# A streaming encoder layer: the sources of three output projections transposed by VectorE and DMA in place of TensorE

## What is computed

```python
def retention_out(o, rg, g_ret, w_ret_o):
    o = rmsnorm(o, g_ret)...                    # per head
    return einsum('btv,vd->btd', silu(rg) * o, w_ret_o)

def diff_out(o, g_sub, lam_init, w_diff_o, dtype):
    o = rmsnorm(o, g_sub) * (1.0 - lam_init)
    return einsum('btv,vd->btd', o, w_diff_o)

def gated_merge(x, y_r, y_d, gr, gd, w_out):
    m = sigmoid(gr) * y_r + sigmoid(gd) * y_d
    return x + einsum('btd,de->bte', m, w_out)
```

## Time and profile before

| | |
|---|---|
| median of 3 runs | 1012.54 us |
| profiled execution, its own time | 1012.54 us |
| its span | 1010.4 us |
| TensorE busy | 990.2 us |
| VectorE busy | 689.5 us |
| ScalarE busy | 509.1 us |
| GpSimd busy | 149.7 us |
| mean granted clock of TensorE | 0.991 |

### The profile page before, as it was taken

One profiled execution on the slowest core, in us unless ns is written; L12 is line 12 of the kernel. 1 busy time (PEld: TensorE's weight loads), 2 busy tenths in 40 slices (PEclk: granted clock), 3 DMA queues, 4 the chain that ended last, 5 costly groups with the idle time before them and its releaser, 6 DMA issues.

```text
span 1010.4 us, 12083 instructions
## 1 busy us (share of the span) xinstructions
PE 990.2 (98%) x4614; PEld 812.8 (80%) x4614; DVE 689.5 (68%) x1003; ACT 509.1 (50%) x680; POOL 149.7 (15%) x184
## 2 busy tenths in 40 slices
PE   9989999999999999999999999999999999999995
PEld 6878888887887888877878888889788888888884
DVE  6699886237656664443448457687889889888893
ACT  6523233335545553332352304554588687887782
POOL 1000001112120301221130000022012122121111
PEclk9999999999999999999999999998999999999998
DMA  9489888882551732553285245137899999999994
GB/s 350 138 250 316 236 222 227 270 247 101 195 192 69 262 114 77 194 204 127 97 299 186 104 152 228 69 127 281 337 401 403 381 404 391 393 405 380 404 397 80
DMA packets 125987, 245.27 MB, mean 243 GB/s; under 512 B 69072, under 2 KB 69376, under 8 KB 113600
## 3 DMA queue, kind: packets, MB, share of 16 engines
q1 hardware_dynamic: 105520, 172.51, 47.1%
q0 software_dynamic: 20112, 71.37, 21.2%
q10 hardware_dynamic: 288, 0.52, 0.1%
HBM read 203.07 MB, written 52.08 MB: 253 GB/s over the span
## 4 chain that ended last, share of the span: by engine, by line
PE 56%; issue 27%; DVE 6%; POOL 3%; SPq 2%; ACT 2%; DMA 1%; POOLq 0%; ACTq 0%; DVEq 0%
PE ps L478 14%; PE ps L480 14%; PE ps L479 14%; PE ps L1861 3%; PE ps L1862 3%; SPq L586 2%; PE ps L1834 2%; POOL x_exp L855 1%; PE ps L1896 1%; POOL out_y L866 1%; PE ps L2004 1%; PE ps L2020 1%; DVE w_lo L450 1%; PE ps L2011 1%; DMA v_tok<-out_v_new 1%
## 5 line engine op out<-in xcount | busy, mean ns | idle before, releaser
L478 PE MATMUL ps<-w_hi,s_hi 128*128 128x512 f32 x640 | 256.4, 401 | 3.1 <-DVE w_lo L414 2.6
L480 PE MATMUL ps<-w_lo,s_hi 128*128 128x512 f32 x640 | 250.3, 391 | 0.0
L479 PE MATMUL ps<-w_hi,s_lo 128*128 128x512 f32 x640 | 249.9, 390 | 0.0
L478 PEld LDWEIGHTS ps<-w_hi,s_hi 128*128 128x128 f32 x640 | 120.6, 188 | 29.2 <-issue 4.6
L479 PEld LDWEIGHTS ps<-w_hi,s_lo 128*128 128x128 f32 x640 | 120.7, 189 | 25.5 <-issue 1.0
L480 PEld LDWEIGHTS ps<-w_lo,s_hi 128*128 128x128 f32 x640 | 120.5, 188 | 25.6
L1013 ACT ACTIVATE stage<-ps,x_rstd 128x512 f32<-128x512 f32 x64 | 43.6, 688 | 150.8 <-PE ps L480 150.4
L414 DVE TENSOR_TENSOR w_lo<-raw,w_hi 128x2048 fp32r<-128x2048 f32 x40 | 91.6, 2290 | 32.2 <-ACT w_hi L409 31.9
L409 ACT CAST w_hi<-raw 128x2048 fp32r<-128x2048 f32 x40 | 76.1, 1908 | 12.0 <-DMA raw<-in_w_in 6.3
L450 DVE TENSOR_TENSOR lo_x<-raw_x,hi_x 128x2048 fp32r<-128x2048 f32 x32 | 72.5, 2286 | 7.9 <-ACT hi_x L427 7.9
L450 DVE TENSOR_TENSOR lo_x<-raw_x,w_hi 128x2048 fp32r<-128x2048 f32 x32 | 72.6, 2286 | 5.4 <-ACT w_hi L427 5.4
(11 more groups left out here) (308 smaller groups left out, 1833.2 us busy)
## 6 DMA issues: line engine op xcount, KB each, us to landing
raw<-in_w_in SPq DMA_DIRECT2D x30, 1024.0 KB, 10.3
raw_x<-in_w_gate SPq DMA_DIRECT2D x30, 1024.0 KB, 24.7
raw_x<-in_w_down SPq DMA_DIRECT2D x18, 1024.0 KB, 24.0
raw_x<-in_w_up SPq DMA_DIRECT2D x16, 1024.0 KB, 21.5
raw<-in_w_up SPq DMA_DIRECT2D x16, 1024.0 KB, 22.4
raw<-in_w_down SPq DMA_DIRECT2D x14, 1024.0 KB, 23.6
x_slots<-in_c_empty SPq DMA_DIRECT2D x4, 2112.0 KB, 11.3
x_exp<-x_slots POOLq DMA_DIRECT2D x16, 528.0 KB, 13.2
```

The lines of the kernel that those rows point to most:

```text
L478: nc.tensor.matmul(out, s_h, w_h, start=first, stop=False)
L479: nc.tensor.matmul(out, s_l, w_h, start=False, stop=False)
L480: return nc.tensor.matmul(out, s_h, w_l, start=False, stop=last)
```

## The change

- VectorE's `turn_source` transposes a tile (source 3: half a tile) in 32x32 blocks into another buffer (`od_turned`, `ro_turned`; for source 3 `ro`, free by then). ScalarE's `store_source` writes it to a DRAM buffer `src_T` with one DMA for each strip of 32 partitions, so that the tile lies there transposed. GpSimd's `reload_source` reads it back over the tile's own SBUF bytes. `loaded_hi` and `loaded_lo` make the two parts from there, 128x1024 at once.
- Source 1's five tiles are turned in units r = 4, 6, ... 12, stored at r = 5, 7, ... 13, read back from r = 6 on. TensorE has no transposes of sources 1 and 2, and of source 3 only those of the sample tile.
- `gated_ro(t)` moves one slot later, into x = 0, t = 1 up to x = 1, t = 0, each followed by the transpose of its tile. In x = 0 the two weight splits move one slot earlier.
- Source 3's halves are turned and stored in x = 2 and x = 3. `loaded_hi(3, 3)` and `loaded_lo(3, 3)` come after x = 3.
- New waits: VectorE waits for the state stores before the second tile of source 2, and for a buffer's store before its next use; GpSimd's residual loads wait for `s_lo` in place of the transposes, and its gate load for source 1's stores.

The copy of what was read back for tile 2 stands ahead of the lower-half copy of chunk 3. The diff, its core:

```diff
                 sp.wait_ge(state_stored, 32 * H)
+                for t in (3, PT):
+                    sp.wait_ge(src_stored[t], stored_source(2, t))
             elif n > LAST:
...
             dma(o["s_sample"][h], st_out[:, 1, :]).then_inc(state_stored, 16)
+        def reload_source(s, t, half=None):
+            c0, c1 = source_columns(half)
+            pool.wait_ge(src_stored[t], stored_source(s, t, half or 0))
+            dma(source_rows(s, t)[:, c0 // P:c1 // P, :],
+                src_T[s][t * D_MODEL + c0:t * D_MODEL + c1, 0:P if t < PT else SAMPLE]
+                .rearrange("(k p) c -> p k c", p=P)).then_inc(res_in[t], 16)
...
                     store_states(h - 1)
+                if r in range(6, 6 + 2 * TT, 2):
+                    reload_source(1, (r - 6) // 2)
                 if r == 17:
...
         pool.wait_ge(ro_squared, UNITS)
+        for t in (3, PT):
+            pool.wait_ge(src_stored[t], stored_source(1, t))
         load_gate("gr", 0, 4)
...
         dma(w_r[:, :, NG:NG + NE], a["w_expert"][0].rearrange("(k p) c -> p k c", p=P)).then_inc(router_in, 16)
+        for t in range(TT):
+            reload_source(2, t)
         pool.wait_ge(src_ready, 2 * TT)
         load_gate("gr", 1, 2)
         pool.wait_ge(p_evacuated, 2 * TT)
+        for half in range(2):
+            for t in range(PT):
+                reload_source(3, t, half)
         load_residual(0)
         for t in range(1, TT):
-            pool.wait_ge(src_transposed, source_unit(3, t) + 2)
+            if t < PT:
+                pool.wait_ge(slo_ready, source_unit(3, t) + 2)
+            else:
+                pool.wait_ge(src_transposed, 2)
             load_residual(t)
...
                 square_o(UNITS - 2 + r)
+            if r in range(5, 5 + 2 * TT, 2):
+                store_source(1, (r - 5) // 2)
             if r >= 16:
-                source_hi(1, r - 16)
+                loaded_hi(1, r - 16)
             if r >= 1:
                 square_ro(r - 1)
         square_ro(UNITS - 1)
-        source_hi(1, PT)
+        loaded_hi(1, PT)
         root()
...
                 u = source_unit(s, t) + half
-                act.wait_ge(src_transposed, u + 1)
+                act.wait_ge(src_transposed, u - BY_PE + 1)
                 if len(halves) == 1 and half == 0:
                     act.wait_ge(logits_ready, 1)
                 c0 = source_column(s, t, half)
                 nc.scalar.copy(s_hi[:, 4 * half:4 * half + 4, c0:c0 + rows],
                                ps[:, source_bank(u), :].rearrange("p (k c) -> p k c", k=4)[:, :, 0:rows])\
                     .then_inc(shi_ready, 1)
+        def store_source(s, t, half=None):
+            c0, c1 = source_columns(half)
+            act.wait_ge(src_turned, turned_count(s, t, half or 0))
+            if half:
+                act.wait_ge(res_in[t], landed_source(s, t))
+            columns = src_T[s][t * D_MODEL + c0:t * D_MODEL + c1, :]\
+                .rearrange("(j a) (q b) -> q a j b", a=BLOCK, q=STRIPS, b=BLOCK)
+            blocks = turned_source(s, t, c0, c1)
+            for q in range(STRIPS if t < PT else SAMPLE // BLOCK):
+                act.dma_start(columns[q], blocks[q * BLOCK:(q + 1) * BLOCK, :].rearrange("a (j b) -> a j b", b=BLOCK))\
+                    .then_inc(src_stored[t], 16)
+        def loaded_hi(s, t):
+            rows = P if t < PT else SAMPLE
+            if s > 1:
+                wait_out(act, 2 * s - 3, t)
+            act.wait_ge(res_in[t], landed_source(s, t, 1 if s == 3 else 0))
+            nc.scalar.copy(s_hi[:, :, t * P:t * P + rows], source_rows(s, t)).then_inc(shi_ready, 2)
...
             for t in range(TT):
-                if t in (1, 2):
-                    dense_hi(act, 2 * c + 1 + t)
+                if t in ((0, 1) if x == 0 else (1, 2)):
+                    dense_hi(act, 2 * c + 1 + t + (x == 0))
                 if x == 0 and t == 3:
                     open_gate(1)
                 if x == 3 and t == 3:
                     dense_hi(act, LAST)
-                if x % 2 == 1 and t >= 1:
-                    source_hi(2 + x // 2, t - 1)
-                if x == 2 and t == 0:
-                    source_hi(2, PT)
+                if x % 2 == 1 and t >= 2:
+                    loaded_hi(2 + x // 2, t - 2)
+                if x == 2 and t < 2:
+                    loaded_hi(2, 3 + t)
+                if x == 0 and 1 <= t < PT:
+                    store_source(2, t - 1)
+                if x == 1 and t == 0:
+                    store_source(2, 3)
+                    store_source(2, PT)
+                if x >= 2 and t < PT:
+                    store_source(3, t, x - 2)
             lower_half_of(x)
         dense_hi(act, LAST + 1)
+        loaded_hi(3, 3)
         source_hi(3, PT)
...
                                 hi.bitcast(f32), ALU.subtract).then_inc(slo_ready, 1)
+        def loaded_lo(s, t):
+            rows, c0 = P if t < PT else SAMPLE, t * P
+            dve.wait_ge(shi_ready, source_unit(s, t) + 2)
+            hi = s_hi[:, :, c0:c0 + rows]
+            lo = s_lo[:, :, c0:c0 + rows] if t < PT else s_hi[:, :, c0 + rows:c0 + 2 * rows]
+            v.tensor_tensor(lo, source_rows(s, t), hi.bitcast(f32), ALU.subtract).then_inc(slo_ready, 2)
+        def turn_source(s, t, half=None):
+            c0, c1 = source_columns(half)
+            rows = slice(0, P if t < PT else SAMPLE)
+            if s < 3 and t >= 2:
+                dve.wait_ge(src_stored[t - 2], stored_source(s, t - 2))
+            v.transpose(turned_source(s, t, c0, c1)[rows], (od if s != 2 else ro)[rows, t, c0:c1])\
+                .then_inc(src_turned, 1)
...
                 norm_attention((r - 4) // 2)
+                dve.wait_ge(src_ready, (r - 4) // 2 + 1)
+                turn_source(1, (r - 4) // 2)
             if t == PT:
...
                 evacuate_out(x, t)
-                if t in (1, 2):
-                    dense_lo(dve, 2 * c + 1 + t)
-                if x == 0:
-                    gated_ro(t)
+                if t in ((0, 1) if x == 0 else (1, 2)):
+                    dense_lo(dve, 2 * c + 1 + t + (x == 0))
+                if x == 0 and t >= 1 or x == 1 and t == 0:
+                    k = t - 1 if x == 0 else PT
+                    gated_ro(k)
+                    if k == 1:
+                        dve.wait_ge(state_stored, 32 * H)
+                    dve.wait_ge(src_ready, TT + k + 1)
+                    turn_source(2, k)
+                if x >= 2 and t < PT:
+                    dve.wait_ge(p_evacuated, TT * x + t + 1)
+                    turn_source(3, t, x - 2)
                 if x == 2 and t == 3:
                     router_weights()
                 if x == 3 and t == 3:
                     dense_lo(dve, LAST)
-                if x % 2 == 1 and t >= 1:
-                    source_lo(2 + x // 2, t - 1)
-                if x == 2 and t == 0:
-                    source_lo(2, PT)
+                if x % 2 == 1 and t >= 2:
+                    loaded_lo(2 + x // 2, t - 2)
+                if x == 2 and t < 2:
+                    loaded_lo(2, 3 + t)
...
         dense_lo(dve, LAST + 1)
+        loaded_lo(3, 3)
         source_lo(3, PT)
+        dve.wait_ge(slo_ready, source_unit(3, PT) + 2)
         v.memset(rows_out[:, :, D_MODEL + 1 + NE:XW], 0.0)
...
                 u = source_unit(s, t) + half
-                if u == 0:
+                if u == BY_PE:
                     pe.wait_ge(tr_evacuated, len(mixes))
-                if u >= 2:
+                if u >= BY_PE + 2:
                     pe.wait_ge(slo_ready, u - 1)
...
             tile_state(r)
-            if r >= 16:
-                attended_source(r - 16)
-        attended_source(PT)
         def next_source(x, t):
-            if x == 1:
-                pe.wait_ge(src_ready, TT + t + 1)
-                source(2, t, ro[:, t, :])
-            elif x == 3:
+            if x == 3:
                 pe.wait_ge(p_evacuated, TT * x + t + 1)
...
                 dense(1 + x // 2, IN_CHUNKS + x, t, p_ready)
-                if x % 2 == 1 and t >= 1:
-                    next_source(x, t - 1)
-                if x == 2 and t == 0:
-                    next_source(1, PT)
         pe.wait_ge(wrs_ready, 1)
         for n, t in enumerate(ORDER):
             dense(3, IN_CHUNKS + 4, t, p_ready, within=lambda: route(n))
```

More of the change, by code:

```diff
@@ L333, in build @@
     state_ready, state_evacuated, state_stored = sem("state_ready"), sem("state_evacuated"), sem("state_stored")
[L334 removed]
+    src_ready, src_transposed, src_turned = sem("src_ready"), sem("src_transposed"), sem("src_turned")
+    src_stored = [sem(f"src_stored{t}") for t in range(TT)]
     gate_in = [sem(f"gate_in{i}") for i in range(5)]
@@ L542, in source_bank, with turned_source, turned_count, stored_source @@
         return 5 + u % 2
+    BY_PE = source_unit(3, PT)
+    def turned_source(s, t, c0, c1):
+        if s == 3:
+            return ro[:, t, c0:c1]
```

(12 more changed lines are left out.)

14 lines of the change are left out of this document (7 added, 7 removed).

## The result

| | before | after |
|---|---|---|
| median of the runs of this comparison | 1012.41 us (4) | 1027.15 us (4) |
| profiled execution, its own time | 1012.54 us | 1025.51 us |
| its span | 1010.4 us | 1023.6 us |

A forecast was written before the change was run, and what follows sets the result against it. TensorE, busy 990.2 of 1010.4 us, was taken to bound the kernel. 14.0 - 3.7 - 3.6 - 0.5 - 2.9 = 3.3 us less, from 1012.5 to 1009.2 us; range 999 to 1023 us.

The forecast's parts named there:

- What is removed: TensorE: fourteen groups of transposes and the 0.53 us wait at 541.02 go, together 14.0 us less.
- Retention stage at nothing: Retention stage: five VectorE transposes and eighteen ScalarE DMA issues are covered by slack of units, cost nothing.
- ScalarE's issue price: ScalarE's source stores: 0.54 us an issue for half tiles of source 3, 0.65 us for strips of full tiles.
- My second bound: Full-tile strips on ScalarE: up to 1.1 us an issue, at twice the pieces.
- First wait: Second product of w_diff_o's second half: TensorE waits 3.7 us for the sample tile's bank, behind ScalarE's stores and copy.
- dear full strips: Rival, only full strips dear: first wait 7.8 us in place of 3.7, time 1013.3 us; chance 0.13.
- Second wait: Before source 3's sample tile: 3.6 us behind tile 2's reload, then about 0.5 us for the last weight block's split.
- the pair's lower end: Lower end for the waits around source 3's sample tile: 2.5 us, with the reload at 4.0 us.
- Clock: TensorE at granted clock 0.50 after waits: 1.7 us for the first wait, 1.2 us for the second, 2.9 us.
- Heavy issues in source 3: Rival, last w_ret_o chunk: 1.14 us an issue beside weight loads, 15 us more than forecast, 1024 us; chance 0.24.
- Free issues: Rival: ScalarE's issues delay nothing behind them, hardly any of the 14.0 us is lost, 998.7 us; chance 0.20.
- from about 0.8 us an issue: Source 3's stores: the issue price from which the heavy rival decides.

The follow-up runs named there:

- long_rows: Changed kernel with every strip stored as it lies in SBUF, 4 KB runs in place of 128-byte pieces, sources wrong: 1011.85 us, ratio 0.9986.
- late_stores: Changed kernel with ScalarE storing only tile 0 of source 2 before its copy of the sample tile's lower half, tiles 1 to 3 behind it: 1021.32 us.
- fold3: Changed kernel with the last w_ret_o product's lower-half copy moved ahead of the split of source 3's tile 2: 1020.77 us, ratio 1.0078.
- turns_only: Changed kernel with VectorE's block transposes and later gating but no store or reload of a source, sources wrong: 998.09 us, ratio 0.9862.
- the last run: Changed kernel, all stores on ScalarE, every reordering, gate before tile 0's store, last weight block split earlier, two expert loads held for residual rows: 1009.38 us.
- s12_gate: Sources 1 and 2 by DMA, source 3 on TensorE, reordered ScalarE stores, second gate opened ahead of tile 0's store: 1009.73 us, 0.9961 of before.
- s13: Changed kernel with source 2's transposes back on TensorE and gating as before, sources 1 and 3 by DMA: 1025.81 us, ratio 1.0107.
- defer_up: Changed kernel with the first two expert loads held back until the last w_ret_o chunk is done: 1023.29 us, ratio 1.0116.

## Why the prediction was wrong

**What is removed, 14.0 us: right.** Without stores and reloads 14.2 us show. The first output product of the changed kernel starts at 510.00 us, 4.8 earlier, where 5.7 were forecast; 0.8 of the rest is the longer wait for w_lo at the start of the run.

**Retention stage at nothing: right.** No wait of TensorE came there, although single issues were held for up to 6.60 us and one group of four for 11.18 us: nothing urgent stands behind them in that stage. The cover was said to be slack of units, and it was. That the issues would be short there wasn't so. (The prediction counts fifteen reloads; the kernel has eighteen.)

**ScalarE's issue price, 0.54 and 0.65 us: the step that failed.** The medians are 0.53 and 0.63, so the price in quiet was right. The error was to use it as the price of each issue. My second bound, 1.1 us, was worked out from the number of pieces in quiet; the row for busy queues, up to 4.49 us and a median of 1.79, lay beside it and was set aside with the argument that these issues have a queue of their own. They have (q10), and it was held all the same. At 14.57 us for eight issues the mean is 1.82 us, near the busy median of the earlier trace rows, though that is of strips with half as many pieces. The trace of before even has a like store that took 7.57 us to issue, while the median of its group is 0.51 us:

```profile
L586 SPq DMA_DIRECT2D zT_q<-turned x40: 306/508/7572, 115.9 to 160.6; - x40
```

So the long tail was there to be read before the run.

**First wait, 3.7 us: measured 8.5.** Place, chain and releaser are as forecast (evacuation of the sample tile, lower-half copy behind ScalarE's stores). In it 5.2 us of issues for tiles 0 and 1 were 14.57. (The upper bound is off in itself: eight issues at 0.45 us more make 7.3 us, not 7.8, and 1012.8 in place of 1013.3 for the rival of dear full strips.)

**Second wait, 3.6 and 0.5 us: measured 5.4, and 5.9 in two before it.** The 5.4 us are the forecast mechanism; taking away just the order that it names took them away. Not in the forecast's sum are 1.6 and 4.3 us, behind stores that are held in the last w_ret_o chunk (of the eight from 594.17 one takes 3.04 us, of the four from 606.26 one 6.62). Of the 0.5 us for the last weight block nothing showed. (By its own terms the pair's lower end is 2.7 us, not 2.5.)

**Clock, 2.9 us: measured about 6,** for three slow stretches, of 1.7 to 2.2 us each, in place of two. The price of one was right.

**The rivals.** "Heavy issues in source 3" gave 1024 us and the right side, with a chance of 0.24. It adds its 15 us to a forecast that already has 4.1 us of waits in the same place, so by its own terms it is nearer 1020. Its place was only half right: it charged 1.14 us for every issue, but the issues are quick again (1.97 us for four) when the loads have passed, and the first chunk is hit as hard. "Free issues", 998.7 us, describes the run without DMAs, 998.1 us, and nothing else. The point "from about 0.8 us an issue" can't be judged: the mean of source 3's 32 issues is 0.88 us, but four of them, of 2.2 to 6.6 us, make half of their sum.

**The rules weighed.** The Trainium skill, "DMA: Bandwidth & Descriptors", section "Issuing engines are not separate DMA queues", has the time to initiate a DMA as usually small beside the DMA itself. By that rule the forecast's ScalarE term would have been too large. The trace agrees at the median (0.53 us to issue, 1.7 us and more to land) and not for the held issues: the one of 6.62 us landed 11.7 us after its start. Its section "Specifications" asks for 512 bytes or more. By that rule the small pieces should be dear, and the trace agrees: 4.4% of the engines' time against 2.2% for the same bytes in long rows, and 15 us of the kernel's time. (The prediction has a strip hold its queue as long as a 1 MB load does; in the trace of before the medians on SyncE are 0.51 and, for the loads of w_in, 0.38 us.)

**Chances.** Slower got 0.25. The two cases in which the issues were dear, 0.24 and 0.13, were treated as separate, while one cause, other transfers beside the stores, makes both at once. Together they give about 1028 us (1024, with 4.1 more from the first wait). That 1027.15 was measured is in part luck: put right as above, the two give about 1024, and the heavy rival gets there with a price on every issue, where a few long ones did it.

What is shown and what isn't: that the small pieces make the holds is shown by long_rows, that the holds cost the first wait through the order on ScalarE by late_stores, that the 5.4 us come from the copy's place behind a reload by fold3, and that nothing but stores and reloads costs time by turns_only. Open stays how much of a hold is a limit on what one queue may have under way and how much the other transfers' share of the engines; no run varied one without the other.

## What to carry to other kernels

Price a DMA issue by what else is on the engines at that moment, not by its median, and look at the longest issue of a row and not only at the middle one. Then ask what stands behind it in the same queue: held stores cost nothing in the retention stage and 8.5 us in front of one copy of 0.58 us. Work that is taken off the bounding engine shows only if every due time near it, gates and buffers too, moves with it; source 1 gained nothing until the gating moved. When moving a transfer out of the way, look for who now lands behind it.

## What the runs showed of the hardware

- Stores in pieces of 128 bytes hold the queue of whichever engine issues them. On GpSimd two strips of 1024 pieces go out in 1.56 us and the next two 4.3 us later; on ScalarE holds of 3.9 and 4.1 us, and up to 6.6 us (8.4 in the last run), come between short ones. The same bytes in long rows are issued in 0.80 us at most.
- A hold doesn't need megabyte loads beside it: 3.26 us with nothing but the change's own stores and reloads of 512 KB under way (s12_gate).
- Ten times the packets for the same 7.34 MB (54624 against 5472) take twice the engines' time, 4.4 against 2.2%, not ten times.
- A store of 64 KB, landed in 1.7 us at best, took up to 12.8 us beside six megabytes of loads; a load of 256 KB, asked for 5 us after four megabytes, took 15.4 us.
- A wait of 2.0 to 8.8 us was mostly followed by some 3 to 6 us of work at the lower clock (0.50), and three times by none: after 2.2 us in s13, 3.5 us in defer_up and 2.7 us in the last run, where the granted clock is 1.00 throughout from 500 to 660 us.
